# Third and fourth weight sums of the gate and up quads: written by VectorE instead of by ScalarE negations and adding transfers

## What is computed

```python
def swiglu(h, w_gu, w_down):
    gu = h @ w_gu
    g, u = jnp.split(gu, 2, axis=-1)
    return (jax.nn.silu(g) * u) @ w_down
```

## Time and profile before

| | |
|---|---|
| median of three runs (lowest to highest) | 1955.8 us (1955.07 to 1957.76) |
| the profiled execution | 1952.36 us, span 1950.6 us |
| TensorE busy | 1883.7 us, 97% of the span |
| VectorE busy | 1450.2 us, 74% |
| ScalarE busy | 1210.0 us, 62% |
| GpSimd busy | 272.4 us, 14% |
| TensorE's waits for ScalarE's copy of product 1 (L3026), in the second half | 5, 8.1 us in all, longest 2.1 |
| TensorE's waits for VectorE's adds to `X` (L3145) | 7, 6.3 us in all, longest 1.2 |
| `raw<-sums` transfers of 512 KB, issue to landing | 20, median 5.6 us |
| `raw<-raw` transfers of 512 KB, issue to landing | 20, median 5.1 us |

### The profile page before, as it was taken

One profiled execution on the slowest core, in us unless ns is written; L12 is line 12 of the kernel. 1 busy time (PEld: TensorE's weight loads), 2 busy tenths in 40 slices (PEclk: granted clock), 3 DMA queues, 4 the chain that ended last, 5 costly groups with the idle time before them and its releaser, 6 DMA issues.

```text
span 1950.6 us, 26707 instructions
## 1 busy us (share of the span) xinstructions
PE 1883.7 (97%) x10258; PEld 1582.1 (81%) x10258; DVE 1450.2 (74%) x1826; ACT 1210.0 (62%) x1786; POOL 272.4 (14%) x339
## 2 busy tenths in 40 slices
PE   5999999999999999999999999999999999999997
PEld 4668768888888888858889899897777779989896
DVE  6677699998999999872557866869444557776868
ACT  4443268888888888844346655657555546655565
POOL 3111210122211101020011011111011111011011
PEclk9999999999999999999999999999999999999999
DMA  8465579999999999962326686775321225777773
GB/s 302 161 216 195 180 260 372 366 378 376 377 377 365 362 369 369 338 220 74 108 66 157 157 199 169 164 187 146 106 65 53 78 76 110 176 191 190 178 169 115
DMA packets 221004, 415.50 MB, mean 213 GB/s; under 512 B 14762, under 2 KB 95543, under 8 KB 219850
## 3 DMA queue, kind: packets, MB, share of 16 engines
q1 hardware_dynamic: 181296, 343.73, 49.5%
q0 software_dynamic: 31008, 59.38, 15.8%
q10 hardware_dynamic: 8570, 10.64, 1.6%
HBM read 381.30 MB, written 24.65 MB: 208 GB/s over the span
## 4 chain that ended last, share of the span: by engine, by line
PE 71%; DVE 11%; DMA 8%; ACT 5%; issue 4%; POOL 1%; ACTq 0%; POOLq 0%; DVEq 0%
PE ps L448 68%; DVE wlo L393 3%; DMA raw<-in_ffn_w_gu 3%; DMA raw<-sums 3%; ACT whi L363 2%; PE ps L2411 1%; DMA raw<-in_ffn_w_down 1%; DVE sums L286 1%; DVE X L3145 1%; ACT raw L255 1%; PE ps L2438 1%; DMA VR<-in_b_subln 1%; DVE ATl L3127 1%; DVE XN L3157 0%; PE ps L3428 0%
## 5 line engine op out<-in xcount | busy, mean ns | idle before, releaser
L393 DVE TENSOR_TENSOR wlo<-raw,whi 128x1024 fp32r<-128x1024 f32 (+1 forms) x638 | 749.2, 1212 | 136.0 <-ACT whi L363 131.6
L363 ACT ACTIVATE whi<-raw 128x1024 fp32r<-128x1024 f32 (+1 forms) x638 | 639.4, 1046 | 232.5 <-PE ps L448 122.3
L448 PE MATMUL ps<-whi,ATh 128*128 128x512 f32 x308 | 121.0, 393 | 6.3 <-DVE X L3145 6.3
L448 PE MATMUL ps<-wlo,ATh 128*128 128x512 f32 x308 | 120.1, 390 | 0.0
L448 PE MATMUL ps<-whi,ATl 128*128 128x512 f32 x308 | 120.0, 390 | 0.0
L448 PE MATMUL ps<-whi,XT0h 128*128 128x512 f32 x256 | 102.9, 402 | 1.7 <-DVE XT0l L2494 1.7
L448 PE MATMUL ps<-whi,XT1h 128*128 128x512 f32 x256 | 102.8, 402 | 1.5 <-DVE XT1l L2494 1.5
L448 PE MATMUL ps<-hT3h,whi 128*128 128x256 f32 (+1 forms) x352 | 103.6, 294 | 0.6 <-DVE hT3l L445 0.6
L448 PE MATMUL ps<-hT5h,whi 128*128 128x256 f32 (+1 forms) x352 | 103.2, 293 | 0.6 <-DVE hT5l L445 0.6
L448 PE MATMUL ps<-hT3l,whi 128*128 128x256 f32 (+1 forms) x352 | 103.4, 294 | 0.0
L448 PE MATMUL ps<-hT3h,wlo 128*128 128x256 f32 (+1 forms) x352 | 103.4, 294 | 0.0
(11 more groups left out here) (529 smaller groups left out, 4894.0 us busy)
## 6 DMA issues: line engine op xcount, KB each, us to landing
raw<-in_w_expert_gate SPq DMA_DIRECT2D x64, 1024.0 KB, 7.3
raw<-in_w_expert_up SPq DMA_DIRECT2D x64, 1024.0 KB, 8.1
raw<-in_w_expert_down SPq DMA_DIRECT2D x64, 1024.0 KB, 6.9
raw<-in_ffn_w_gu SPq DMA_DIRECT2D x44, 1024.0 KB, 7.5
raw<-in_ffn_w_down SPq DMA_DIRECT2D x16, 1024.0 KB, 9.6
raw<-in_ada_w SPq DMA_DIRECT2D x24, 512.0 KB, 4.8
raw<-in_ffn_w_gu POOLq DMA_DIRECT2D x20, 512.0 KB, 5.9
raw<-sums POOLq DMA_DIRECT2D x20, 512.0 KB, 5.6
```

Of the source, the lines that this page charges most:

```text
L363: e.activation(hi[:, c], x, ACT.Copy).then_inc(self.S("w_hi"), 1)
L393: e.tensor_tensor(lo[:, c], raws[h], hi[:, c].bitcast(F32), ALU.subtract).then_inc(self.S("w_lo"), 1)
L448: return e.matmul(o, l, r, start=start, stop=stop, skip_group_check=True)
```

## The change

For the 20 narrow quads sums 3 and 4 are written by one VectorE subtraction each, straight from `sums` and the raw blocks (`third`, `fourth`). The negations of `first` and of the total by ScalarE, and the two adding transfers by POOL, are gone for them. The wide quads stay as they are. Sums 1 and 2 stay in all quads.

The core of the diff (the changed thresholds of semaphores elsewhere only recount what is left):

```diff
         of = {1: (first, None), 5: (over, 1), 6: ((None, first[1]), 2), 3: (right, None), 7: (first, 3), 2: (low, None), 4: (over, 4)}
         for p in order:
             (i, at), t = of[p]
-            made[p] = self.split(name, i, a, 512 if at is None else 256,
-                                 after=None if t is None else (self.S(f"sum{t}"), (q + 1) * (1 if t == 2 else 16)), at=at)
+            after = None if t is None else (self.S(f"sum{t}"), (q + 1) * (1 if t == 2 else 16))
+            if t in (3, 4):
+                after = self.rest(q, t, wide=at is None)
+            made[p] = self.split(name, i, a, 512 if at is None else 256, after=after, at=at)
...
+    def rest(self, q, t, wide):
+
+        before = sum(1 for items, _, _ in self.quads[:q] if items[0][1] is None)
+        if wide:
+            return self.S(f"sum{t}"), 16 * (before + 1)
+        return self.S(f"rest{t}"), q - before + 1
+
+    def negations(self, q):
+        return sum(3 if items[0][1] is None else 1 for items, _, _ in self.quads[:q])
+
+    def total_used(self, e, q):
+
+        e.wait_ge(*self.lowered(self.quads[q][2][6]))
+        if self.wide(q):
+            e.wait_ge(self.S("negated"), self.negations(q) + 3)
+            e.wait_ge(*self.rest(q, 3, True))
+        else:
+            e.wait_ge(*self.rest(q, 4, False))
+
+    def third(self, e, q):
+
+        _, _, made = self.quads[q]
+        x = self.block(q, 0)[0]
+        e.wait_ge(*self.lowered(made[1]))
+        e.wait_ge(self.S("sum2"), q + 1)
+        e.tensor_tensor(x, self.total(q)[0], x, ALU.subtract).then_inc(self.S("rest3"), 1)
+
+    def fourth(self, e, q):
+
+        items, _, made = self.quads[q]
+        e.wait_ge(*self.lowered(made[5]))
+        e.wait_ge(*self.loaded(items[2][0]))
+        e.tensor_tensor(self.block(q, 1)[0], self.block(q, 2)[0], self.total(q)[0], ALU.subtract).then_inc(self.S("rest4"), 1)
 
...
             first = up_pieces(l, 1)[0]
             q = 13 * l
             W.high(e, first + 2)
-            W.negate_first(e, q)
             for k in range(2):
                 e.wait_ge(*R.full(f"fg{l}", k))
                 e.activation(FA[:, k, :], R.bank(f"fg{l}", k)[:, :], ACT.Silu).then_inc(*R.free(f"fg{l}", k))
             for i in range(4):
                 sum_high(i)
                 if i == 0:
-                    W.negate_total(e, q)
                     W.high(e, first + 3)
...
                             W.negate_over(e, q + 1)
-                        if m == 3 and f < fn - 2:
-                            W.negate_first(e, q + 1)
-                        if m == 5 and f < fn - 2:
-                            W.negate_total(e, q + 1)
                         if m == 1 and f == 4:
...
                 if f0 + fn < 22:
                     W.negate_over(e, q)
                     W.high(e, js[6] + 3)
-                    W.negate_first(e, q)
-                    W.negate_total(e, q)
                 else:
...
             sum_low(3)
+            W.third(e, q)
+            W.fourth(e, q)
             n = 1
...
+                        if m == 4 and f < fn - 2:
+                            W.third(e, q + 1)
+                        if m == 6 and f < fn - 2:
+                            W.fourth(e, q + 1)
                         if m == 5 and f == fn - 2:
                             W.add_total(e, q + 1)
...
                         if m < 6:
                             W.low(e, js[6] + (3 if m == 4 else 5))
+                    W.third(e, q)
+                    W.fourth(e, q)
                 else:
...
             for q in range(13 * l, 13 * l + 13):
                 if q % 13 > 0:
                     W.add_first(e, q)
-                W.add_rest(e, q)
+                if W.wide(q):
+                    W.add_rest(e, q)
```

More of the change, by code:

```diff
@@ L281, in add_total @@
         if before >= 0:
-            e.wait_ge(self.S("negated"), 3 * before + 3)
-            e.wait_ge(self.S("sum3"), 16 * (before + 1))
-            e.wait_ge(*self.lowered(self.quads[before][2][6]))
+            self.total_used(e, before)
         for out_, x, y in zip(self.total(q), self.block(q, 3), self.block(q, 1)):
@@ L293, in add_first @@
         first = self.items[i] if at is None else self.items[i][:, at * a:(at + 1) * a, :]
-        e.wait_ge(self.S("negated"), 3 * q + 1)
+        e.wait_ge(self.S("negated"), self.negations(q) + 1)
         e.dma_start(self.block(q, 1, False)[0].rearrange("p (c n) -> p c n", c=a), first, accum_op=ALU.add).then_inc(self.S("sum1"), 16)
@@ L299, in add_rest @@
         items, _, _ = self.quads[q]
-        e.wait_ge(self.S("negated"), 3 * q + 2)
+        e.wait_ge(self.S("negated"), self.negations(q) + 2)
         e.wait_ge(self.S("sum2"), q + 1)
         e.dma_start(self.block(q, 0, False)[0], self.total(q, False)[0], accum_op=ALU.add).then_inc(self.S("sum3"), 16)
-        e.wait_ge(self.S("negated"), 3 * q + 3)
+        e.wait_ge(self.S("negated"), self.negations(q) + 3)
         e.wait_ge(*self.loaded(items[2][0]))
@@ L3309, in distance_pool @@
         def distance_pool(e):
-            e.wait_ge(S("negated"), 3 * 13)
-            e.wait_ge(S("sum3"), 16 * 13)
+            e.wait_ge(S("negated"), W.negations(13))
+            e.wait_ge(*W.rest(12, 3, True))
             e.wait_ge(*W.lowered(W.quads[12][2][6]))
@@ L3873, in _ @@
             W.load(e, len(W.items))
-            e.wait_ge(S("negated"), 3 * 26)
-            e.wait_ge(S("sum3"), 16 * 26)
+            e.wait_ge(S("negated"), W.negations(26))
+            e.wait_ge(*W.rest(25, 3, True))
             e.wait_ge(*W.lowered(W.quads[25][2][6]))
```

## The result

The changed kernel takes 1960.4 us (median of 20 runs, 1953.6 to 1968.3) against 1955.0 for the kernel before (20 runs beside them, 1948.7 to 1960.6). The ratio is 1.0029 with a 95% interval of 1.0017 to 1.0041: **slower by 5.7 us, 3.3 to 8.0**. The profiled execution took 1964.43 us, with a span of 1962.7.

The account below looks back on a forecast made before the run. TensorE, busy 97% of the span, was taken as the bound, with late moments deciding. Heads +2.5, +1.6, +0.1 and units -0.7 gave +3.5; clock +2.0 made +5.5 on the median 1955.8, about 1961.4, range 1955.5 to 1965.0.

Parts of the forecast that it names:

- Group heads: Four gate/up groups after a down quad: third sum queued on VectorE, TensorE restarts 10.66 after add_total starts (S), +2.5 us.
- S itself doesn't move: At the group heads, add_total's start S stays, hanging on the down product's adds and the first sum's kept transfer.
- First layer's head: Third sum stands behind sum_low(3), so product 6 restarts at 1040.49 against 1038.95: new wait, +1.6 with slow first matmul.
- Second layer's head: Same chain as at the first layer gives a gap of 1.54 against 1.41: +0.1 us.
- Units: Between the heads, ScalarE no longer waits for `raw<-sums`, so two small TensorE gaps close: -0.7 us.
- Down products: Feed-forward down stages, VectorE busy 43 of 50 us: no term in the forecast's sum.
- a loss by a rival: VectorE becomes the bound in the down products: up to 1 us each, six places, +6 on top; inside a 7%.
- The clock: Second layer's two group heads grow past 2 us; two clock falls in three chances at 1.5 each, +2.0 us.
- The 3.4 us between profile and median: Profile 1952.4, median 1955.8; a rival said earlier timed runs already had two clock falls, giving 1959.0, 13%.
- Busy times: Whole kernel: 40 subtractions put 46 us more on VectorE, 40 removed negations take 42 us off ScalarE.
- The queue theory: From the experiments: third sum behind other VectorE work at layer and group heads makes gaps, longer ones lose clock; explains +5.7.
- that of load: From the experiments: VectorE with 41 us more is late in many places, the units too; rival explanation of +5.7.

## Why the prediction was right

The forecast, 1961.4, against 1960.4 measured, and +5.5 against +5.7: sign and size came out. By its own steps:

- **Group heads, restart at S + 10.66.** Measured S + 10.56 at all four. The named wait is there, for the third sum. But the term was +2.5 and the means of four profiles say +1.7 (the gaps sum to 7.80 and 9.54). 4 x 0.1 of that is the chain. The other 0.4 is the step "S itself doesn't move", which failed: product 6 is due on average at S + 8.08 before and at S + 8.17 after, 0.3 of it at the second head (S + 7.82 and S + 8.16). It goes with who writes the head's own sums: S + 8.26 in the kernel with only the heads changed, S + 7.83 in that with the heads as before. The one profile that the sum was made on hid this: its gaps sum to 7.43, the least of the four, because its first and third heads were due 0.1 to 0.3 later than in the others.
- **First layer's head, +1.6.** Measured 1.48 in all four profiles, and 0.10 for the slow first matmul. **Second layer's head, +0.1:** 1.42 became 1.48.
- **Units, -0.7.** What lies outside heads, down products and clock fell by 0.55, most of it the one slow transfer above. The timed kernel with only these units changed can't tell it from nothing.
- **Down products, given 0 here and a loss by a rival.** This is the missed term: they lose 2.0 less (7.7 and 5.7). The load of VectorE could have made them worse, and did not, since the 14 units' subtractions lie outside them. 1.4 of the 2.0 lies at one place, the second layer's middle down product: the four profiles of before lose 2.0 to 2.7 there, three of the changed kernel 0.8 and one 1.3. The prediction had seen a late third sum in the unit ahead (1794.42) and priced it at 0.35. But ScalarE, held up by it for 2.0 to 2.3 us, also negates `over` of the wide quad late. The transfer of that quad's first sum is then issued 1.5 us later against TensorE's products, and ScalarE waits 4.7 to 5.4 us for it. Rows of before, and one of the changed kernel at the same place:

```profile
1788.97 1.06 ACT L363 ACTIVATE whi<-raw 128x1024 fp32r<-128x1024 f32 x1 [2.34 <-DMA raw<-sums]
...
1804.79 2.01 ACT L363 ACTIVATE whi<-raw 128x1024 fp32r<-128x1024 f32 x2 [4.70 <-DMA raw<-in_ffn_w_down]
...
1827.42 0.50 PE L448 MATMUL ps<-whi,ATh 128*128 128x512 f32 x1 [1.14 <-DVE X L3145]
```

```profile
1814.75 2.01 ACT L397 ACTIVATE whi<-raw 128x1024 fp32r<-128x1024 f32 x2 [3.33 <-PE ps L482]
```

The kernel with only the heads changed and the one with the copy made three times keep the transfers of these units and lose 0.8 there, so a small shift in time is enough, and which part of the change makes it is open. The rest, some 0.5, goes with a wait of VectorE ahead of a wide quad's total (`raw<-in_ffn_w_down`): once or twice in each profile of before, 0.8 to 2.0 us in all, and in none of the changed kernel's. That wait isn't for the first sum: in the first profile it ends as SyncE's load of the block `right` lands (1090.58), and the first sum had landed at 1086.92. The kernel with only the heads changed has it and loses 6.1 in its down products, the one with the heads as before doesn't have it and loses 5.6.

- **The clock, +2.0.** Mis-sized by the profiles, and open. Over four profiles each, slow matmuls went from 3.4 to 3.8, +0.35. The two second-layer heads grew to 2.23 to 2.51 as worked out, but lost the clock in 2 of 8 cases, not in two of three. Both of these were in the first profile. The timed runs say more. Each has a mean granted clock on record: 0.9931 over the 20 of the changed kernel, 0.9949 over the 52 of before that were timed beside the experiments (those timed beside the changed kernel have none on record). In the earlier trace rows a mean of 0.77 over 7.35 us, 0.23 x 7.35 = 1.7, cost 1.5 us. So 0.0018 over 1955 us is, as an estimate, 3.5 x 1.5 / 1.7 = 3.1 us, wherever in the kernel it was lost. For the kernel with only the heads changed it is 0.9930 against 0.9952 beside it, 3.8 of its 5.3 us. The rule of the Trainium skill, "TensorE: Matmul & The Clock Gate", Part 1 (the throttle's windows run free of the program), fits: equal gaps fare differently from run to run, as the 2.47 and the 2.41 above.
- **The 3.4 us between profile and median.** The profile of before lay at the fast end because of what comes ahead of the feed-forwards (92.0 us lost, the lowest of all), not because of falls that it lacked: it had two falls, the others of before two, none and none. The rival that drew on this gap had the wrong cause.
- **Busy times.** VectorE +41 where I counted 46, ScalarE -34 where I counted 42. Busy time counts the overlap of two instructions back to back once (0.08 us on VectorE, 0.09 on ScalarE), and with the change 84 more of VectorE's instructions and 75 fewer of ScalarE's start without a gap.

**The cause.** Heads alone carry the loss (+5.3), the same work in an earlier place takes it away and 14 us more, and the other units cost nothing that shows. The queue theory stands, that of load falls.

**What stays open.** The profiles' means put +1.1 us into the feed-forwards (+3.3 at the heads, +0.4 of clock, -2.0 in the down products, -0.6 elsewhere), and 20 timed runs say +3.3 to +8.0. Within one kernel the sum varies by up to 5.6 us from profile to profile and the part ahead by up to 8.6, so four profiles each don't exclude the timed figure, but they leave 2 to 7 us of the measured loss unlocated. With the estimate of 3.1 for the clock in place of 0.4 the sum is +3.9; where the timed runs lose that clock no profile shows. That the +5.5 met the +5.7 so closely is partly luck: the group heads' term was 0.8 too high, the down products' gain of 2.0 was missing, and the clock's term may have been too low.

## What to carry to other kernels

When an operation replaces a transfer, price it by where it stands in its engine's queue and not by its own duration: 1.2 us of work ended 7 us after the total was begun, and was no faster than a transfer of 5.6, and the same subtraction written directly behind its input turned a loss of 5.7 us into a gain of 14.3. Look at heads of stages separately from the steady state, since there the same line stands behind other work. And before two single profiles are compared, look at a stretch that the change doesn't touch: here it held 9.5 of 12.1 us.

## What the runs showed of the hardware

- Between the dense matmuls of the feed-forwards, after 34 gaps of 2.05 to 2.56 us the granted clock fell 16 times, after 30 gaps of 1.39 to 1.83 us never, after two of 2.83 and 2.84 not, after two of 3.49 and 3.73 both times. At the same place and the same length it differs from run to run. A fall costs some 1.5 us beyond the gap, in the longest 2.5.
- The first matmul after such a gap takes 0.10 us longer also when the clock stays up (0.39 against 0.28 in the rows).
